# Attention weights divided by their sum before they are turned, and value rows as the fixed operand of the product

## The reference, cut to what matters

```
sc = q.k / sqrt(128) + c[t] - c[s], and -inf where s > t        (forgetting attention)
p  = softmax(sc);  o = p @ v
sc = q.mk / sqrt(128);  p = softmax(sc);  o = p @ mv            (memory attention, 256 keys)
```

## Time and profile before

| | us |
|---|---|
| three runs: median (lowest, highest) | 1722.36 (1719.72, 1726.2) |
| profiled execution, its own time | 1722.07 |
| span of the profile (first to last instruction) | 1720.3 |
| mean granted TensorE clock | 0.991 |

### The profile page before, as it was taken

One profiled execution on the slowest core, in us unless ns is written; L12 is line 12 of the kernel. 1 busy time (PEld: TensorE's weight loads), 2 busy tenths in 40 slices (PEclk: granted clock), 3 DMA queues, 4 the chain that ended last, 5 costly groups with the idle time before them and its releaser, 6 DMA issues. The chain is left out here.

```text
span 1720.3 us, 26344 instructions
## 1 busy us (share of the span) xinstructions
PE 1641.9 (95%) x10771; PEld 1568.1 (91%) x10771; DVE 845.3 (49%) x1239; ACT 533.3 (31%) x895; POOL 518.7 (30%) x388
## 2 busy tenths in 40 slices
PE   5999999999999999979999999999999999998999
PEld 4989998999999999979989899999989999888976
DVE  5666653333344331680077673345657551885611
ACT  6322343222222222222244443321145222653300
POOL 1334416334334312811245552122211211102400
PEclk9999999999999999989999999999999999999999
DMA  4212144222222114333266452235210332434521
GB/s 152 51 25 53 50 131 143 69 56 69 69 68 68 50 50 132 120 86 99 74 184 179 123 181 74 85 120 154 68 37 16 109 99 70 145 112 130 151 88 56
DMA packets 189365, 163.19 MB, mean 95 GB/s; under 512 B 18380, under 2 KB 157055, under 8 KB 188726
## 3 DMA queue, kind: packets, MB, share of 16 engines
q1 hardware_dynamic: 189246, 161.51, 32.1%
HBM read 131.38 MB, written 30.22 MB: 94 GB/s over the span
## 5 line engine op out<-in xcount | busy, mean ns | idle before, releaser
L276 POOL TENSOR_TENSOR wL<-w_raw,wH 128x1024 fp32r<-128x1024 f32 (+1 forms) x113 | 242.7, 2148 | 828.4 <-ACT wH L269 828.2
L301 PE MATMUL ps<-hH,wH 128*128 128x344 f32 x1920 | 449.1, 341 | 19.6 <-DVE hL L462 5.5
L301 PE MATMUL ps<-hL,wH 128*128 128x344 f32 x1920 | 411.0, 321 | 0.0
L301 PE MATMUL ps<-hH,wL 128*128 128x344 f32 x1920 | 409.9, 320 | 0.0
L301 PEld LDWEIGHTS ps<-hH,wH 128*128 128x128 f32 x1920 | 313.1, 190 | 32.9 <-issue 18.5
L301 PEld LDWEIGHTS ps<-hL,wH 128*128 128x128 f32 x1920 | 325.3, 189 | 0.0
L301 PEld LDWEIGHTS ps<-hH,wL 128*128 128x128 f32 x1920 | 323.0, 189 | 0.0
L269 ACT ACTIVATE wH<-w_raw 128x1024 fp32r<-128x1024 f32 (+1 forms) x116 | 108.5, 935 | 118.7 <-PE ps L301 112.2
L2828 POOL TENSOR_SCALAR fa_logits<-fox_c_bc,token_scalars 128x128 f32<-128x128 f32 (+7 forms) x32 | 61.5, 1922 | 58.4 <-DMA fox_c_bc<-rows_g_c_beta 30.1
L1796 ACT ACTIVATE d_m<-ps 128x512 f32<-128x512 f32 x48 | 28.6, 595 | 142.3 <-PE ps L1972 142.3
L301 PE MATMUL ps<-branch_in_r,wH 128*128 128x344 f32 x288 | 61.9, 324 | 0.0
(11 more groups left out here) (573 smaller groups left out, 2795.5 us busy)
## 6 DMA issues: line engine op xcount, KB each, us to landing
w_raw<-in_w_in SPq DMA_DIRECT2D x80, 512.0 KB, 5.0
m_th<-gate_spill SPq DMA_DIRECT2D x28, 516.0 KB, 4.6
gate_spill<-d_gate SPq DMA_DIRECT2D x18, 516.0 KB, 3.0
fa_kv<-in_cache_fox_k SPq DMA_DIRECT2D x32, 256.0 KB, 3.1
fa_kv<-in_cache_fox_v SPq DMA_DIRECT2D x32, 256.0 KB, 3.6
w_raw<-in_w_branch SPq DMA_DIRECT2D x32, 256.0 KB, 2.8
gate_spill<-fa_gate SPq DMA_DIRECT2D x10, 516.0 KB
x_rows<-in_x_prompt SPq DMA_DIRECT2D x8, 512.0 KB, 5.8
```

The source lines that it names most:

```text
L276: pool.tensor_tensor(self.wL[:, t % 2, 0:nk], self.raw_at(t)[:, 0:nk], self.wH[:, t % 2, 0:nk].bitcast(F32), ALU.subtract).then_inc(self.w ...
L301: last = pe.matmul(self.ps[:, b + g, 0:cols], w[:, t % 2, k], x[:, k, g * cols:(g + 1) * cols], start=(k == 0 and n == 0), stop=(k == nk - ...
```

## The change

DVE inverts the sum of tile n and then multiplies the whole row of weights of tile n by it, in place, before PE turns them. The turn of tile n now waits for this multiply (semaphore `od`) instead of the exponential. In DVE's queue `invert_sum(n)` moves ahead of `logits(n+2)`. In the value product the two operands change places: value rows are the fixed operand and the turned weights stream, so that the result comes with the head's width on the partitions, as the branch buffer wants it. `divide`, `turn_back`, the buffer `_o_rows`, the semaphore `b` and the two turnings back left to the next projection are gone; `out(n-1)` stands in ACT's queue where `divide(n-1)` stood, and the values of the next tile wait for it.

```diff
                 def turn(u):
                     n, b0, k = units[u]
-                    pe.wait_ge(N["exp"], n + 1)
+                    pe.wait_ge(N["od"], n + 1)
...
                     pe.wait_ge(N["pTe"], u + 1)
-                    if n >= 1 and b0 == 0:
-                        pe.wait_ge(N["od"], n)
-                    if n >= 2 and b0 == 0:
-                        pe.wait_ge(N["oe"], n - 1)
+                    if n and b0 == 0:
+                        pe.wait_ge(N["oe"], n)
                     for b in range(k):
-                        last = pe.matmul(VO, PT[:, u % 2, b], V[:, b0 + b, h],
+                        last = pe.matmul(VO, V[:, b0 + b, h], PT[:, u % 2, b],
                                          start=(b0 + b == 0), stop=(b0 + b == nb[n] - 1))
...
-                def turn_back(n):
-                    pe.wait_ge(N["od"], n + 1)
-                    if n >= 1:
-                        pe.wait_ge(N["oe"], n)
-                    pe.transpose(BO, OQ[:, n % 2], K.ident[:]).then_inc(N["b"], 1)
...
-                K.owed = {1: lambda pe: turn_back(len(its) - 2), 4: lambda pe: turn_back(len(its) - 1)}
...
                 def invert_sum(n):
                     dve.wait_ge(N["exp"], n + 1)
                     dve.reciprocal(RS[:, n % 4:n % 4 + 1], RS[:, n % 4:n % 4 + 1]).then_inc(N["rs"], 1)
+                    dve.wait_ge(N["rs"], n + 1)
+                    w = LG[:, n % NL, 0:nb[n] * P]
+                    dve.tensor_scalar(w, w, RS[:, n % 4:n % 4 + 1], None, ALU.mult).then_inc(N["od"], 1)
...
                 for n in range(len(its)):
+                    invert_sum(n)
                     if n + 2 < len(its):
                         logits(n + 2)
-                    invert_sum(n)
...
-                def divide(n):
-                    act.wait_ge(N["v"], of_tile[n][-1] + 1)
-                    act.wait_ge(N["rs"], n + 1)
-                    if n >= 1:
-                        act.wait_ge(N["b"], min(n, len(its) - 1))
-                    act.activation(OQ[:, n % 2], VO, ACT.Identity,
-                                   scale=RS[:, n % 4:n % 4 + 1]).then_inc(N["od"], 1)
                 def out(n):
                     h, t = its[n]
-                    act.wait_ge(N["b"], n + 1)
-                    act.activation(Q(h, slice(t * P, (t + 1) * P)), BO, ACT.Identity
+                    act.wait_ge(N["v"], of_tile[n][-1] + 1)
+                    act.activation(Q(h, slice(t * P, (t + 1) * P)), VO, ACT.Identity
                                    ).then_inc(N["oe"], 1)
```

More of the change, by code:

```diff
@@ L2706, in attend @@
         PT = sb("_pT", [P, 2, UB, P])
-        OQ = sb("_o_rows", [P, 2, P])
         NM, RS = sb("_negmax", [P, 4]), sb("_sum", [P, 4])
@@ L2711, in attend @@
         N = {x: K.sem(tag + "_" + x) for x in ("rel", "s", "lg", "max", "exp", "rs", "pT",
-                                               "pTe", "v", "od", "b", "oe")}
+                                               "pTe", "v", "od", "oe")}
         KV = sb("_kv", [P, 2, NP, H, P])
@@ L2737, in attend @@
         TB = 5
-        VO, BO = K.ps[:, 6, 0:P], K.ps[:, 6, P:2 * P]
+        VO = K.ps[:, 6, 0:P]
         decode_out = lambda: Q(slice(None), slice(SEQ, TOK)).rearrange("p h b -> p b h")
@@ L2939, in _ @@
                         if u == of_tile[n][0]:
-                            if n >= 2:
-                                turn_back(n - 2)
                             decode_values(n, 2)
@@ L3142, in _ @@
                         if n >= 1 and u == of_tile[n][0]:
-                            divide(n - 1)
-                            if n >= 2:
-                                out(n - 2)
+                            out(n - 1)
                         if u == of_tile[n][0]:
@@ L3152, in _ @@
                 K.split_hi(act, END + 1)
-                divide(len(its) - 1)
-                out(len(its) - 2)
                 out(len(its) - 1)
```

## The result

The changed kernel takes 1778.33 us (median of 4 runs, 1775.44 to 1779.18) against 1721.37 for the kernel before on the same chip: ratio 1.0324, 95% interval 1.0303 to 1.0345, so slower by 57 us. The forecast was 1767, range 1735 to 1795. In the profiled execution the span is 1776.7 us against 1720.3: +56.4.

The account below looks back on a forecast made before the run. PE's order of work bounds both attentions (PE busy 95%, VectorE 49%). Terms 30.2 (fa) + 5 (clock) + 10.2 (ma with its end) = 45.4 on 1722.07 gave 1767 us, range 1735 to 1795.

Parts of the forecast that it names:

- fa, lateness: Prompt attention: turns wait for VectorE's late multiply, cluster by cluster, adding up to 34.0 us, less 3.8 for transposes: +30.2.
- fa, clock: Prompt attention: PE at granted clock 0.50 after three long new waits (tiles 6, 14, 30); +5 us (0 to 8).
- between the attentions: Between and behind the attentions PE is busy nearly all the time, so nothing there takes a shift back.
- ma, loop: Memory attention: turns wait on VectorE's queries, decode keys and multiplies, a two-tile loop taking 5.2 or 6.65 us; 16.3 us in all.
- end, with its clock: End of memory attention: without the last turning back, final product starts earlier, -3.4 us, and the slow clock goes, -2.7.
- rival 1: VectorE's rows stay put, so a wait is paid once, at fa's tile 14 (9.8 us late); 1725 us, chance 0.08.
- The transposes: Turning back removed: 64 transposes, 32 per attention, at 0.12 us each, 7.7 us of PE, 3.8 in fa.
- Rival 2: Multiplies held by GpSimd's bias and weight subtraction, some 15 meetings at 1 us each; 1783 us, chance 0.12.
- The multiply: VectorE's added multiply per tile: 0.27 to 0.74 us for 128 to 1024 columns, 0.34 in ma, start 0.2.
- The value product: With V fixed, as many products and weight loads as before: 0 us, bounds some 8 us either way.

Follow-up runs that it names:

- E5: Changed kernel with 393 identity transposes put on TensorE ahead of fa and ma turns that waited 1 us or more, the wait itself kept; 1768.9 us.
- E1: Changed kernel without its division: no multiply, the turn waits for the exponential, VectorE in its old order, output not the reference's; 1711.5 us.
- E11: Kernel before, with only the very last turning back of the second attention moved ahead of the third projection step, not the fifth; 1715.5 us.
- E7: Changed kernel with division of tile n+1 ahead of tile n's decode work, turn and value products one tile later, a fourth logits buffer; 1729.6 us.

## Why the prediction was right, and where it was short

The direction, the mechanism and most of the places were as written; the sum was 11 us short. The turns waited 29.1 us in fa and 25.5 in ma, where some 35 and 20 were forecast. Of the four tiles named as the largest in fa, tile 23 was not: its 2.09 us lie below those of tiles 2, 13, 16 and 20. The table measures by how far a turn lies behind the same turn before, in the profiled executions. E5, the filled-waits run, gives the part without the clock, as far as its fa is free of clock loss (1.7 us are left):

| term | forecast | measured |
|---|---|---|
| fa, lateness | +30.2 | +33.1 (E5, first turn to last) |
| fa, clock | +5 | +6.0 (39.1 - 33.1) |
| between the attentions | 0 | -1.2 |
| ma, loop | +16.3 | +24.6, of it 4.4 clock (24.6 - 20.2 in E5) |
| end, with its clock | -6.1 | -6.1 |
| sum | +45.4 | +56.4 |

*Lateness of fa.* Cluster by cluster, without the clock (E5): tile 2 +1.5 (forecast 2.1), tiles 6 to 8 +4.9 (5.4), 13 to 16 +15.0 (9.8 + 3.3), 20 to 23 +6.9 (6.1), 28 to 30 +5.5 (5.1). They add up, as the prediction said, and rival 1, by which the shift would have stopped at 9.8, falls (it also counted 6.3 for the end, where the forecast has 6.1): in the changed kernel the turn of tile 16 is 24.0 us late, the last 39.1. The transposes were worth 1.8 and not 3.8 (E1).

*Between the attentions.* The trace before has a granted clock of 0.50 from 1284 to 1287 us (1.7 us of loss), which the changed kernel's trace lacks; this is enough for the -1.2. Why it is there in some runs and not in others stays open.

*The step that failed: the size of ma's loop.* Its logic held. Of the eight pairs of tiles from one decode key to the next, the one without a projection step and without a disturbance took 5.2 us (forecast 5.2), the undisturbed one with a step 6.7 (6.65), the one with the gate's product 6.8 (6.3), the one behind the query load 6.9 (6.8). The other four were disturbed. By stretch, ma's turns fell behind by 2.0 us up to tile 3 (forecast 3.3), 14.8 from there to tile 19 (9.4), 0.6 to tile 21 (-0.7) and 7.2 to the last (4.3). The term was mis-sized by 8.3 in all, for two reasons that I had priced at nothing in ma:
- The clock. I looked for it only behind waits of about 5 us like that of the earlier trace rows. But waits of 2.2 to 3.4 us in ma were followed by a granted clock of 0.50 at tiles 2, 5, 15, 19 and 24 (not so the 2.9 us at tile 13). E5 puts this at 4.4 us; as one of its batches outlasted its wait (the pair to tile 13 took 8.0 there, 6.8 in the changed kernel), nearer 5.6.
- Meetings of VectorE with GpSimd. Two key products, beside GpSimd's weight subtraction, took 2.08 and 1.98 us where the others took 1.22, and one multiply (tile 24) 2.24 where 31 took 0.35 or 0.36: 3.5 us in all. The key products were not new: they took 2.36 and 2.27 before, where no turn waited for them. The prediction quoted the first and then gave every key step of the loop the undisturbed length. The multiply and GpSimd's weight subtraction beside it, in the changed kernel:

```profile
1582.07 2.24 DVE L2968 TENSOR_SCALAR ma_logits<-ma_logits,ma_sum 128x256 f32<-128x256 f32 x1
```
```profile
1581.53 2.63 POOL L276 TENSOR_TENSOR wL<-w_raw,wH 128x1024 fp32r<-128x1024 f32 x1 [35.35 <-ACT wH L269]
```

The multiply ends at 1584.31, GpSimd at 1584.16, so by these rows it could not end before GpSimd did. The Trainium skill (SBUF — State Buffer, "SBUF: two separate sides") says that of a VectorE operation in a two-port mode and a GpSimd operation the one that starts first keeps the ports that they share for its whole instruction, and the other is blocked. The trace agrees at this row, though no run shows in which mode the multiply runs. It does not agree everywhere: of the 20 multiplies that ran beside a GpSimd row 7 were longer than others of their width, by 4.8 us in all, and 13 kept their length. Rival 2 had 15 meetings at 1 us each: it was right in kind, for at most a third of its price.

*The multiply.* 0.29 to 0.75 us undisturbed (forecast 0.27 to 0.74), 0.35 in ma (0.34); the start alone 0.21 (0.2). The value product changed nothing, as costed (E1). *The end* came out at the forecast -6.1, in part by luck: the wait is 3.1 us shorter (5.16 to 2.04) for a forecast 3.4, and the other 3.0, its slow clock, was put at 2.7. E11 moves that turning back alone and gains 5 us.

*Clock of fa.* That the forecast of 5 is close to the 6.0 paid is luck, two mistakes against each other: I expected three slow stretches and there were seven (15.4 us of loss), and of the 13.7 us that E5 took away more than half had been hidden.

*Two readings.* Half of 5.6 us is 2.8, not 2.7. And in the trace before GpSimd's bias rows last up to 4.2 us, not 2.9; this bears on rival 2 alone. Neither moves the forecast by more than 0.1.

## What to carry to other kernels

Before a product is made to wait for a second engine, compare, tile by tile, when the product runs with when that engine's queue gets to the work: an engine 49% busy over the kernel can be more than a tile behind in the stage that matters. If the work must go there, put it in the queue ahead of side work, above all of work that itself waits for DMAs (39 of 57 us here), and look for another engine for it (11 more). Removing a wait can move it: when the turn no longer waited for VectorE (E7), the scores and the decode products waited longer.

## What was not expected of the hardware

Waits of TensorE of 2 us were already followed by its low clock at times: behind 2.09 us at fa's tile 23 the granted clock was 0.50, while behind 2.84 us at tile 2 it stayed at 1.0. And a slow clock is not paid in full where the engine would have waited soon: with the waits filled, 22 us less of clock loss in the attentions gave back 10 there, and 8 in the kernel's time.
